# A two-layer diffusion trunk: bias rows laid by the host, counts in five products, gate and residual ahead of the last sums, output in halves from SP, keys moved into a wait

## The chip, the cores and the metric

One core of a Trainium2 chip runs the whole program. Its engines are TensorE (PE in the rows; PEld is its load of weights), VectorE (DVE), ScalarE (ACT), GpSimd (POOL) and SyncE (SP, which only issues transfers and waits). All share 16 DMA engines. The metric is the device time of one execution in microseconds; lower is better.

## What is computed

Two groups of tokens (128 context, 256 latent, together three tiles of 128) go through two layers with shared weights. Cut to what matters here:

```python
mod = silu(cond) @ w_mod + b_mod           # shift1, scale1, gate1, shift2, scale2, gate2
h = x * (1 + scale1) + shift1
a = gmlp(h @ w_in); b = hyena(h @ w_in)    # b: a long convolution by way of spectra
m = attention(h @ w_in)                    # keys: compressed latents @ mla_wukv, and a rotary part
x = layer_norm(ALPHA * x + gate1 * (concat(a, b, m) @ w_out))
h = x * (1 + scale2) + shift2              # then top-1 of 4 groups, top-2 of its 8 experts
x = layer_norm(ALPHA * x + gate2 * moe(h))
```

The outputs are x of both groups and, of each layer, the compressed keys of the context tokens.

## The kernel before

Nothing schedules the program: each engine's order is written out by hand, in one function an engine, and semaphores join them. Everything is float32; a product is two records on TensorE in the trace.

**Weights.** SP streams chunks of 1 MB (`w_mod`, `w_in`, `w_out`) through a ring of four places; a place comes free when TensorE has used it (`chunk_done`). In the expert stage it streams 48 chunks of 2 MB a layer through five slots; a slot comes free when TensorE (`done`) has used it and VectorE and ScalarE have copied a part of it (`copied_d`, `copied_a`).

**Start.** TensorE multiplies the first eight `w_mod` chunks, between them the small products of the filter networks (`filter_hidden`), which VectorE and ScalarE finish. VectorE then adds `b_mod`, loaded by ScalarE's queue into four partition rows of `mod_sums`, to the sums (`add_group(0)`), normalises the third tile of x, shapes the filter taps (`filter_taps`), and TensorE turns those into spectra (L604). ScalarE stores the sums to DRAM, and GpSimd reads them back as broadcast rows for `modulated`.

**Attention.** `keys(g)` (L751) makes the keys of two heads from `ckvT`. In both layers keys 0 and 1 stand behind `forward(1)`, keys 2 and 3 behind `inverse(1)`, ahead of the queries (L796). `inverse` (L746) waits for VectorE.

**Router.** VectorE picks two experts a token. TensorE counts, with a triangular and an all-ones matrix, how many earlier tokens chose each expert (L921), and all tokens (L924). From that VectorE makes the places (`pick`), and TensorE gathers the rows of each expert group (L938).

**Experts.** They come in four octs. In each, `gate_up` (L959) multiplies eight chunks, ScalarE applies silu, VectorE multiplies (`gate`, L1955), TensorE turns the blocks (`turns`), ScalarE copies them out (L1381, L1383), and `down` (L959) multiplies four chunks in two halves of 512 columns. ScalarE and VectorE split the result in a high and a low part (`y_high`, `y_rest`), `scatter` (L1047) brings them back to token order, and VectorE adds them to `moe` (`summed`, L1989). The down chunks of an oct are used among the gate chunks of the next; those of the last oct stand alone (`last_oct_work`). VectorE also copies the chosen parts of each chunk (`copy(c)`, L1949) in between.

**End of a layer.** Tile by tile VectorE multiplies `moe` by the gate (L2178), adds ALPHA x (L2179), takes the statistics (L1535 to L1538), and with ScalarE's square root and row scaling (`norm`, L1225) in between applies the next modulation in layer 0, or the last gain and bias in layer 1 (L1551, L1552). GpSimd stores the three tiles of x (L564).

A branch, taken when an expert has very many tokens, works off the rest of them; with these inputs the other side runs.

Of the kernel before, what the change touches and what calls it, by code (L numbers as in the profile page):

```python
# [199 lines left out]
def build(nc, a, outs):  # L200
# [126 lines left out]
    for name in ("x_in", "cond_in", "mlp_in", "taps_in", "dft_in", "cT", "mod_zero", "bmod_in", "mod_sum", "mod_out", "mod0_out",  # L327
                 "ln_var", "ln_std", "ln_scale", "normed", "pool_step", "x0", "chunk_done", "small_in", "cache_in",
                 "mod12_in", "gate_in", "ln_in", "dve_step", "state_out", "y_out", "h_hi", "h_lo", "h_saved"):
# [50 lines left out]
    def _(sp):  # L380
# [8 lines left out]
        for l in range(DEPTH):  # L389
# [41 lines left out]
            with sp.If(units >= P + 1):  # L431
# [11 lines left out]
                sp.wait_ge(r["multiplied"], REST_MUL * ROUNDS * OCTS)  # L443


    @block.gpsimd
    def _(pool):
# [113 lines left out]
        for t in range(TT):  # L561
            pool.wait_ge(s["x2"], at("x2", DEPTH - 1, t + 1))
            dst = outs[0][0] if t == 0 else outs[1][0, (t - 1) * P:t * P]
            pool.dma_start(dst, x[:, t, :]).then_inc(s["y_out"], 16)  # L564
        pool.wait_ge(s["state_out"], 16 * 2 * DEPTH)
        pool.wait_ge(s["h_saved"], 16 * DEPTH)
        pool.wait_ge(s["y_out"], 16 * TT)
# [3 lines left out]
    def _(pe):  # L571
# [80 lines left out]
        for l in range(DEPTH):  # L652
# [97 lines left out]
            def keys(g):  # L750
                pe.matmul(ps[g][:, :], wukv[:, P * g:P * (g + 1)], ckvT, start=True, stop=True).then_inc(s["k_raw"], 1)  # L751
# [22 lines left out]
            for t in range(4):  # L774
                mm = pe.transpose(ps[1][0:QK, t * P:(t + 1) * P], kpeb[:, t, :], ident)
# [31 lines left out]
            def scores(hh):  # L807
                b = 2 * (hh % 2)
                pe.wait_ge(s["kT"], at("kT", l, 2 if hh == 0 else 4))
# [50 lines left out]
            keys(2)  # L860
            keys(3)
# [57 lines left out]
            for t in range(TT):  # L919
# [278 lines left out]
    def _(act):  # L1198
# [324 lines left out]
    def _(dve):  # L1523
# [111 lines left out]
        for l in range(DEPTH):  # L1635
# [437 lines left out]
            def last_oct_work():  # L2073
# [11 lines left out]
                for i in range(3, BLOCKS):  # L2085
                    y_rest(last_oct, i)
# [214 lines left out]
```

## Time and profile before

| | us |
|---|---|
| median of three runs | 1203.7 |
| the three runs | 1197.64, 1203.7, 1204.4 |
| the profiled execution | 1202.92 |
| its span, first to last instruction | 1201.1 |
| TensorE busy in the span | 1016.5 (85%) |
| VectorE busy | 543.5 (45%) |
| ScalarE busy | 349.3 (29%) |
| read from HBM | 303.11 MB, 257 GB/s |

The times below are from the start of the span. A busy share is a mean over stages; what a change is worth is read at the place where it acts. A row names line, engine, operation, the tile written and those read, the shape, how many records, and in brackets how long the engine was idle before and what ended that.

### The profile page before, as it was taken

How to read it: one execution, taken by the hardware profiler on the slowest of the kernel's cores; microseconds unless marked ns; L12 is line 12 of the kernel's file. 1: busy time of each engine (PE TensorE's matmuls, PEld its weight loads, DVE VectorE, ACT ScalarE, POOL GpSimd, SP SyncE). 2: the span in 40 equal slices, each digit the busy share in tenths (PEclk: the TensorE clock that was granted, in tenths of full speed). 3: DMA queues.
4: the chain of work that ended last, by engine and by line, in shares of the span. 5: the costliest groups of instructions: out<-in, count | busy, mean ns of one | idle time of the engine just before them, and what ended most of it. 6: DMA issues, size and time to landing. Idle time of an engine off the chain costs nothing.

```text
span 1201.1 us, 19792 instructions
## 1 busy us (share of the span) xinstructions
PE 1016.5 (85%) x8178; PEld 600.0 (50%) x8178; DVE 543.5 (45%) x1218; ACT 349.3 (29%) x731; POOL 87.5 (7%) x97
## 2 busy tenths in 40 slices
PE   3768878899977999999986899799959999999970
PEld 2447548765444644435332757565445545344330
DVE  5450033468464234251467615677463242432446
ACT  3120000336131342333242122345122433333331
POOL 1110000010140000000001600000230000000000
PEclk8579988999977999899997899899968999998995
DMA  9865768850356869899986314010486699999941
GB/s 343 320 262 208 294 277 298 327 195 19 140 219 241 348 278 422 337 403 387 424 356 237 140 62 150 12 53 22 168 292 254 244 374 422 367 419 357 408 178 53
DMA packets 48620, 309.52 MB, mean 258 GB/s; under 512 B 6428, under 2 KB 6685, under 8 KB 15749
## 3 DMA queue, kind: packets, MB, share of 16 engines
q1 hardware_dynamic: 39516, 274.08, 57.3%
q0 software_dynamic: 7856, 31.85, 7.5%
q10 hardware_dynamic: 1144, 2.19, 0.6%
q8 instruction: 68, 1.11, 0.4%
q14 instruction: 36, 0.29, 0.1%
HBM read 303.11 MB, written 4.98 MB: 257 GB/s over the span
## 4 chain that ended last, share of the span: by engine, by line
PE 68%; DVE 13%; DMA 11%; ACT 3%; issue 3%; ACTq 1%; SPq 0%; DVEq 0%; POOL 0%
PE bank L959 20%; PE bank L938 9%; PE bank L853 7%; PE bank L694 5%; PE bank L1047 5%; PE bank L680 4%; DMA arena<-in_b_mod 4%; PE bank L705 3%; DMA ring<-in_w_in 2%; DMA ring<-in_moe_gate_up 2%; PE bank L746 2%; PE bank L604 2%; DMA ring<-in_w_mod 2%; PE bank L621 1%; PE bank L796 1%
## 5 line engine op out<-in xcount | busy, mean ns | idle before, releaser
L938 PE MATMUL bank<-sel,h_hi 128*128 128x384 f32 x192 | 83.8, 436 | 9.4 <-DVE sel L1917 9.4
L621 PE MATMUL bank<-ring,arena 128*32 128x64 f32 x3072 | 58.9, 239 | 31.8 <-DMA ring<-in_w_mod 21.4
L853 PE MATMUL bank<-ring,act_t 128*128 128x512 f32 x192 | 84.1, 594 | 0.0
L938 PEld LDWEIGHTS bank<-sel,h_hi 128*128 128x128 f32 x192 | 64.4, 335 | 29.5 <-issue 23.3
L938 PE MATMUL bank<-sel,h_lo 128*128 128x384 f32 x192 | 78.9, 411 | 0.0
L1369 ACT ACTIVATE arena<-bank 128x384 f32<-128x384 f32 x64 | 31.4, 491 | 160.2 <-PE bank L938 160.2
L959 PE MATMUL bank<-ring,arena 128*32 128x512 f32 x480 | 62.4, 640 | 16.5 <-DVE act_t L1955 11.3
L621 PEld LDWEIGHTS bank<-ring,arena 128*32 128x32 f32 x3072 | 52.4, 122 | 45.0 <-issue 22.2
L694 PE MATMUL bank<-act_t,ring 128*128 128x384 f32 x192 | 65.7, 504 | 3.8 <-DMA ring<-in_w_in 3.8
L1047 PE MATMUL bank<-y_hi,selT 128*128 128x512 f32 x144 | 61.7, 428 | 7.0 <-DVE y_lo L1978 6.7
L938 PEld LDWEIGHTS bank<-sel,h_lo 128*128 128x128 f32 x192 | 65.2, 340 | 0.0
L1978 DVE SCALAR_TENSOR_TENSOR y_lo<-bank,region_v,y_hi 128x512 fp32r<-128x512 f32 x48 | 34.6, 748 | 57.3 <-ACT y_hi L1391 57.3
L853 PEld LDWEIGHTS bank<-ring,act_t 128*128 128x128 f32 x192 | 35.8, 190 | 43.6 <-issue 43.6
L1047 PE MATMUL bank<-y_lo,selT 128*128 128x512 f32 x144 | 56.8, 394 | 0.0
L1955 DVE TENSOR_TENSOR act_t<-bank,act_t 128x256 f32<-128x256 f32 x24 | 8.9, 419 | 104.7 <-ACT act_t L1377 104.6
L959 PE MATMUL bank<-arena 128*32 128x512 f32 x416 | 52.0, 598 | 3.1 <-DVE arena L1949 3.1
L1391 ACT ACTIVATE y_hi<-bank,region_v 128x512 fp32r<-128x512 f32 x48 | 31.0, 680 | 75.2 <-PE bank L959 75.2
L694 PEld LDWEIGHTS bank<-act_t,ring 128*128 128x128 f32 x192 | 37.6, 197 | 30.5 <-DMA ring<-in_w_in 4.2
L1047 PEld LDWEIGHTS bank<-y_hi,selT 128*128 128x128 f32 x144 | 26.9, 187 | 50.9 <-DVE y_lo L1978 30.9
L680 PE MATMUL bank<-ring,act_t 128*128 128x256 f32 x192 | 43.9, 391 | 3.8 <-DMA ring<-in_w_in 2.2
L1617 DVE TENSOR_TENSOR arena<-arena,bank 128x512 f32<-128x512 f32 x6 | 4.1, 685 | 87.2 <-PE bank L621 76.4
L959 PE MATMUL bank<-region_k,arena 128*32 128x512 f32 x352 | 42.4, 599 | 0.0
(310 smaller groups left out, 1758.3 us busy)
## 6 DMA issues: line engine op xcount, KB each, us to landing
ring<-in_moe_gate_up SPq DMA_DIRECT2D x60, 1024.0 KB, 8.8
ring<-in_w_mod SPq DMA_DIRECT2D x48, 1024.0 KB, 9.2
region_k<-in_moe_gate_up SPq DMA_DIRECT2D x44, 1024.0 KB, 8.1
ring<-in_moe_down SPq DMA_DIRECT2D x32, 1024.0 KB, 9.5
arena<-in_moe_down SPq DMA_DIRECT2D x28, 1024.0 KB, 9.2
arena<-in_moe_gate_up SPq DMA_DIRECT2D x20, 1024.0 KB, 9.9
ring<-in_w_in SPq DMA_DIRECT2D x10, 1024.0 KB, 7.7
ring<-in_w_out SPq DMA_DIRECT2D x8, 1024.0 KB, 5.2
```

The source lines that it names most:

```text
L604: mm = pe.matmul(ps[SPEC_BANKS[l][b][part]][:, :], dft[:, o:o + P], src[:, t, :], start=(i == 0), stop=(i == len(tiles) - 1))
L621: mm = pe.matmul(ps[MOD_BANK[g]][32 * j:32 * j + 32, c * 64:c * 64 + 64], cT[:, k, :], w[:, k, j * 64:j * 64 + 64], start=(k == 0), stop=( ...
L680: mm = pe.matmul(ps[t][:, c * 256:(c + 1) * 256], act_t[:, k, t * P:(t + 1) * P], w[:, k, :], start=(k == 0), stop=(k == K8 - 1))
L694: mm = pe.matmul(ps[3 + c % 4][:, 0:TOK], w[:, k, c % 2 * P:c % 2 * P + P], act_t[:, k, :], start=(k == 0), stop=(k == K8 - 1))
L705: mm = pe.matmul(ps[t][:, c0 - 1280:c0 - 1280 + n], act_t[:, k, t * P:(t + 1) * P], w[:, k, :], start=(k == 0), stop=(k == K8 - 1))
L853: mm = pe.matmul(ps[2 * t + half][:, :], act_t[:, 2 * c + k, t * P:(t + 1) * P], w[:, k, half * 512:(half + 1) * 512], start=(c == 0 and k ...
L938: mm = pe.matmul(ps[gather_bank(o, k)][:, 0:TOK], src[:, t, k:D:K8], sel[:, t, :, :].rearrange("p v n -> p (v n)"), start=(t == 0 and i == ...
L959: return pe.matmul(out[r, :], stationary[:, r], moving, start=start, stop=stop, tile_position=(0, UNIT * j), skip_group_check=True)
L1047: mm = pe.matmul(ps[SUM_BANKS[t]][:, :], selT[:, v, t * P:(t + 1) * P], y[:, n % 2, :], start=(v == 0 and j == 0), stop=(v == 2 and j == 1 ...
L1369: act.activation(xg[:, first:first + VISITS, k, :], ps[gather_bank(o, k)][:, 0:TOK].rearrange("p (v n) -> p v n", n=P), ACT.Copy)\
L1391: act.activation(y_hi[:, n % 2, :], ps[4 + n % 2][:, :], ACT.Copy, scale=column(o, i % VISITS)).then_inc(e["y_high"], 1)
L1978: dve.scalar_tensor_tensor(y_lo[:, n % 2, :], ps[4 + n % 2][:, :], rt[:, weight:weight + 1], y_hi[:, n % 2, :].bitcast(F32), ALU.mult, ALU ...
```

## The change

**1. Bias rows.** The host lays `b_mod` out as four rows of 3072 numbers. Two DMAs with 4 rows each take the place of four DMAs with 96 runs of 64 numbers each.

**2. Counts.** One triangular product for tile 0; one all-ones product of tile i for all later tiles and the total at once (96, 64, 32 columns, the moving operand repeated); one triangular product for tiles 1 and 2.

**3. Gate and residual.** `folded(t)` multiplies what is summed so far (three octs) by the gate and adds ALPHA x, among the last gate chunks of oct 3. The last oct's sums are multiplied by the gate as they leave the bank, and `residual` adds them to x in halves. The statistics of the first half are taken before the sums of the second.

**4. Output.** In layer 1 the last gain and bias run in halves (`last_affine`), and SP stores each half tile.

**5. Keys.** In layer 1 alone keys 0 and 1 move ahead of `inverse(0)`, keys 2 and 3 to where 0 and 1 were, all in banks 0 and 1; the rotary part goes through bank 7. ScalarE copies keys 0 and 1 out before `signal_out(1)`.

```diff
-        for l in range(DEPTH):
-            bview = a["b_mod"][l].rearrange("(b j n) -> j b n", j=4, n=64)
-            for c in range(2):
-                act.dma_start(mod_sums[c:P:32, l * 1536:(l + 1) * 1536].rearrange("p (b n) -> p b n", n=64),
-                              bview).then_inc(s["bmod_in"], 16)
+        for c in range(2):
+            act.dma_start(mod_sums[c:P:32, :], a["b_mod"]).then_inc(s["bmod_in"], 16)
...
-            for t in range(TT):
-                for i in range(t + 1):
-                    pe.matmul(ps[7][:, t * EXPERTS:(t + 1) * EXPERTS], tri if i == t else ones, chosen[:, i, :],
-                              start=(i == 0), stop=(i == t))
+            counts = ps[7][:, 0:(TT + 1) * EXPERTS].rearrange("p (t n) -> p t n", t=TT + 1)
+            pe.matmul(counts[:, 0, :], tri, chosen[:, 0, :], start=True, stop=True, skip_group_check=True)
             for i in range(TT):
-                mm = pe.matmul(ps[7][:, TT * EXPERTS:(TT + 1) * EXPERTS], ones, chosen[:, i, :], start=(i == 0), stop=(i == 2))
+                pe.matmul(counts[:, i + 1:TT + 1, :], ones, chosen[:, i:i + 1, :].to_broadcast([P, TT - i, EXPERTS]),
+                          start=(i == 0), stop=(i == TT - 1), skip_group_check=True)
+            mm = pe.matmul(counts[:, 1:TT, :], tri, chosen[:, 1:TT, :], start=False, stop=True, skip_group_check=True)
...
+                    if o == OCTS - 1:
+                        last = dve.tensor_tensor(dst, bank[:, :], gates[:, min(t, 1), half * 512:(half + 1) * 512], ALU.mult)
...
+            def folded(t):
...
+                link(dve.tensor_tensor(moe[:, t, :], moe[:, t, :], gates[:, min(t, 1), :], ALU.mult))
+                link(dve.scalar_tensor_tensor(x[:, t, :], x[:, t, :], ALPHA, moe[:, t, :], ALU.mult, ALU.add))
+
+            def residual(t, half):
+
+                cols = slice(half * 512, (half + 1) * 512)
+                dve.wait_ge(e["acc"], SUMS * (OCTS * l + OCTS - 1) + TT * half + t + 1)
+                link(dve.tensor_tensor(x[:, t, cols], x[:, t, cols], moe[:, t, cols], ALU.add))
...
+            def joint(t):
+
+                lnst = st[:, 80 + 14 * t:94 + 14 * t]
+                link(half_stats(t, 1))
+                link(dve.bn_aggr(lnst[:, 12:14], lnst[:, 0:12]))
+                dve.tensor_scalar(st[:, 60 + t:61 + t], lnst[:, 13:14], LN_EPS, None, ALU.add).then_inc(s["ln_var"], 1)
...
+        for t in range(TT):
+            dst = outs[0][0] if t == 0 else outs[1][0, (t - 1) * P:t * P]
+            for half in range(2):
+                cols = slice(half * 512, (half + 1) * 512)
+                sp.wait_ge(s["y_done"], 2 * t + half + 1)
+                sp.dma_start(dst[:, cols], x[:, t, cols]).then_inc(s["y_out"], 16)
+        sp.wait_ge(s["y_out"], 16 * 2 * TT)
...
-            pe.wait_ge(s["latT"], at("latT", l, 2))
+            pe.wait_ge(s["latT"], at("latT", l, 3))
+            if l > 0:
+                keys(0)
+                keys(1)
             inverse(0)
             pe.wait_ge(s["yc"], at("yc", l, 2))
             pe.wait_ge(s["latT"], at("latT", l))
+            if l > 0:
+                pe.wait_ge(s["kT"], at("kT", l, 2))
             signal_turned(1)
             late(l, 3)
             forward(1)
-            keys(0)
-            keys(1)
+            keys(2 * l)
+            keys(2 * l + 1)
```

Three places show what moves. On TensorE the counts of a layer, before (`cst` holds both matrices, `region_v` the choices):

```order
L921 MATMUL bank<-region_v,cst 128x32 [waits oh]
L921 MATMUL bank<-region_v,cst 128x32 x5
L924 MATMUL bank<-region_v,cst 128x32 x3
```

And in the change:

```order
L929 MATMUL bank<-region_v,cst 128x32 [waits oh]
L931 MATMUL bank<-region_v,cst 128x96
L931 MATMUL bank<-region_v,cst 128x64
L931 MATMUL bank<-region_v,cst 128x32
L933 MATMUL bank<-region_v,cst 128x64
```

Nine products become five, three of them wider, and the one wait stays.

On VectorE among the last gate chunks of layer 0, before (a copy is two rows; `small` and `arena` on the left of an L1949 row are its stages, `region_s` is `moe`, L2033 and L2035 prepare the next layer's rows, L1955 is the gate of the last oct):

```order
L2033 TENSOR_TENSOR wukv<-wukv,region_w 128x1024
L1949 REGISTER_ALU [waits e_over,moe_full1,dve_step]
L1949 COPY small<-arena 128x512
L1949 REGISTER_ALU
L1949 COPY small<-arena 128x512
L2035 SCALAR_TENSOR_TENSOR region_q<-region_q,lnr 128x1024
L1949 REGISTER_ALU [waits e_over,moe_full2,dve_step]
L1949 COPY arena<-ring 128x512
L1949 REGISTER_ALU
L1949 COPY arena<-ring 128x512
L1955 TENSOR_TENSOR act_t<-bank,act_t 128x256 [waits e_silu] x3
```

And the same place of the change (line numbers are those of the changed kernel; L2021 and L2022 are `folded`):

```order
L2082 TENSOR_TENSOR wukv<-wukv,region_w 128x1024
L2021 TENSOR_TENSOR region_s<-region_s,arena 128x1024 [waits gate_in,x1,e_acc,dve_step]
L2022 SCALAR_TENSOR_TENSOR x<-x,region_s 128x1024 [waits dve_step]
L1969 REGISTER_ALU [waits e_over,moe_full1,dve_step]
L1969 COPY small<-arena 128x512
...
L2021 TENSOR_TENSOR region_s<-region_s,arena 128x1024 [waits dve_step]
L2022 SCALAR_TENSOR_TENSOR x<-x,region_s 128x1024 [waits dve_step]
L1969 REGISTER_ALU [waits e_over,moe_full2,dve_step]
L1969 COPY arena<-ring 128x512
...
L2021 TENSOR_TENSOR region_s<-region_s,arena 128x1024
L2022 SCALAR_TENSOR_TENSOR x<-x,region_s 128x1024 [waits dve_step]
L1975 TENSOR_TENSOR act_t<-bank,act_t 128x256 [waits e_silu,dve_step]
```

Six operations of 1024 columns now stand ahead of the last gate, two of them ahead of the copy into `small`, four ahead of the copy into `arena`.

On VectorE behind the last scatter of layer 0, before:

```order
L1978 SCALAR_TENSOR_TENSOR y_lo<-bank,region_v,y_hi 128x512 [waits e_y_high,e_w_col] x3
L1989 TENSOR_TENSOR region_s<-bank,region_s 128x512 [waits e_sct] x3
L2158 UNCONDITIONAL_BRANCH
L2178 TENSOR_TENSOR region_s<-region_s,arena 128x1024 [waits ln_in,x1,gate_in,e_acc]
L2179 SCALAR_TENSOR_TENSOR x<-x,region_s 128x1024 [waits dve_step]
```

And in the change:

```order
L1998 SCALAR_TENSOR_TENSOR y_lo<-bank,region_v,y_hi 128x512 [waits e_y_high,e_w_col] x2
L2028 TENSOR_TENSOR x<-x,region_s 128x512 [waits e_acc]
L2028 TENSOR_TENSOR x<-x,region_s 128x512 [waits e_acc,dve_step] x2
L1998 SCALAR_TENSOR_TENSOR y_lo<-bank,region_v,y_hi 128x512 [waits e_y_high,e_w_col,dve_step]
L2032 BN_STATS st<-x 128x6
L2032 BN_STATS st<-x 128x6 [waits dve_step] x2
L2010 TENSOR_TENSOR region_s<-bank,arena 128x512 [waits e_sct,dve_step]
L2010 TENSOR_TENSOR region_s<-bank,arena 128x512 [waits e_sct] x2
L2028 TENSOR_TENSOR x<-x,region_s 128x512 [waits e_acc]
L2028 TENSOR_TENSOR x<-x,region_s 128x512 [waits e_acc,dve_step] x2
L2032 BN_STATS st<-x 128x6 [waits dve_step]
```

The residuals of the first half stand ahead of the last low part, and all three tiles are summed and added before the first statistics are complete; no operation of 1024 columns stands between the sums and the statistics any more.

## Rows read from the trace of the kernel before

**Rows 1.** The page: TensorE's granted clock in 40 slices; the chain by line.

```profile
PEclk8579988999977999899997899899968999998995
...
PE bank L959 20%; PE bank L938 9%; PE bank L853 7%; PE bank L694 5%; PE bank L1047 5%; PE bank L680 4%; DMA arena<-in_b_mod 4%; PE bank L705 3%; DMA ring<-in_w_in 2%; DMA ring<-in_moe_gate_up 2%; PE bank L746 2%; PE bank L604 2%; DMA ring<-in_w_mod 2%; PE bank L621 1%; PE bank L796 1%
```

**Rows 2.** Timeline, VectorE: start us, us, line, operation, idle before.

```profile
48.95 0.69 DVE L1617 TENSOR_TENSOR arena<-arena,bank 128x512 f32<-128x512 f32 x1 [10.77 <-DMA arena<-in_b_mod]
49.55 0.66 DVE L1580 TENSOR_SCALAR arena<-bank,fw 64x384 f32<-64x384 f32 x1
```

**Rows 3.** Timeline, TensorE: the start, and L604 in layer 1.

```profile
41.90 1.54 PE L581 MATMUL bank<-arena,fw 64*64 64x384 f32 x2
...
68.66 11.79 PE L604 MATMUL bank<-region_k,arena 128*128 128x512 f32 x20 [11.12 <-DVE region_k L1599]
...
690.28 8.75 PE L604 MATMUL bank<-region_k,arena 128*128 128x512 f32 x20
```

**Rows 4.** DMA from 13 to 48 us, ScalarE's queue: packets, MB, share.

```profile
q10 hardware_dynamic: 403, 0.11, 1.4%
```

**Rows 5.** Timeline, GpSimd: the modulation rows, the last store.

```profile
52.26 0.53 POOL L468 DMA_DIRECT2D wukv<-mod_rows  x1 [28.19 <-DMA mod_rows<-arena]
...
1191.54 0.53 POOL L564 DMA_DIRECT2D out<-x  x1 [1.86 <-DVE x L1552]
```

**Rows 6.** Transfers to the outputs, 16 to 512 KB, from issue to landing.

```profile
DMA to landing us min/median/max: 1.7/2.9/6.3
```

**Rows 7.** The program's end (L2189): ns min/median/max, start us.

```profile
L2189 SPq DRAIN  x1: 73/73/73, 1169.3 to 1169.3; - x1
...
L2189 POOLq DRAIN  x1: 6194/6194/6194, 1194.7 to 1194.7; - x1
```

**Rows 8.** Timeline, TensorE: router and counts of layer 0.

```profile
353.89 3.63 PE L898 MATMUL bank<-small,act_t 128*128 128x36 f32 x16 [0.69 <-ACT act_t L1346]
362.43 2.77 PE L921 MATMUL bank<-region_v,cst 128*128 128x32 f32 x12 [4.92 <-DVE region_v L1870]
365.01 1.47 PE L924 MATMUL bank<-region_v,cst 128*128 128x32 f32 x6
```

**Rows 9.** Timeline, VectorE: sums behind the last scatter of layer 1, last operation.

```profile
1168.66 1.89 DVE L1989 TENSOR_TENSOR region_s<-bank,region_s 128x512 f32<-128x512 f32 x3 [0.82 <-PE bank L1047]
...
1190.02 1.23 DVE L1552 TENSOR_TENSOR x<-x,lnr 128x1024 f32<-128x1024 f32 x1
```

**Rows 10.** Timeline, VectorE: copies c+10, c+11 and the last gate, layer 0.

```profile
607.81 0.76 DVE L1949 COPY small<-arena 128x512 f32 x2
...
609.83 0.76 DVE L1949 COPY arena<-ring 128x512 f32 x2
...
612.50 1.22 DVE L1955 TENSOR_TENSOR act_t<-bank,act_t 128x256 f32<-128x256 f32 x3 [1.91 <-ACT act_t L1377]
```

**Rows 11.** Timeline, TensorE: `down(3, 0)` and `down(3, 1)` of layer 0.

```profile
615.48 1.92 PE L959 MATMUL bank<-ring,region_w 128*32 128x512 f32 x16 [0.65 <-ACT act_t L1383]
...
618.61 1.92 PE L959 MATMUL bank<-region_k,region_w 128*32 128x512 f32 x16 [0.67 <-DMA region_k<-in_moe_down]
```

**Rows 12.** Timeline, ScalarE: row scaling at layer 1's end.

```profile
1179.32 1.24 ACT L1225 ACTIVATE x<-x,st 128x1024 f32<-128x1024 f32 x1 [4.26 <-DVE st L1545]
```

**Rows 13.** Timeline, all engines: the same place of layer 1.

```profile
1136.14 0.76 DVE L1949 COPY arena<-ring 128x512 f32 x2 [3.78 <-DMA ring<-in_moe_gate_up]
...
1141.02 1.15 ACT L1410 ACTIVATE small<-ring 128x512 f32 x2 [1.64 <-DMA ring<-in_moe_down]
...
1142.98 1.94 PE L959 MATMUL bank<-ring,region_w 128*32 128x512 f32 x8 [2.03 <-ACT act_t L1383]
```

**Rows 14.** Timeline, TensorE: both `inverse`, the queries of layer 1.

```profile
762.91 6.84 PE L746 MATMUL bank<-arena,region_v 128*128 128x128 f32 x24 [4.04 <-DVE region_v L1735]
...
781.44 6.14 PE L746 MATMUL bank<-arena,region_v 128*128 128x128 f32 x24 [2.46 <-DVE region_v L1735]
...
789.13 2.74 PE L796 MATMUL bank<-arena,region_w 128*128 128x384 f32 x8
```

More of the change, by code:

```diff
@@ L858, in w_out @@
                 return mm
-            keys(2)
-            keys(3)
+            if l == 0:
+                keys(2)
+                keys(3)
             pe.wait_ge(s["yc"], at("yc", l))
@@ L1552, in affine, with last_affine @@
             dve.tensor_tensor(x[:, t, :], x[:, t, :], lnr[:, 1, :], ALU.add).then_inc(s[done], 1)
+        def last_affine(base, t):
+            dve.wait_ge(s["normed"], base + t + 1)
+            for half in range(2):
+                cols = slice(half * 512, (half + 1) * 512)
+                link(dve.tensor_tensor(x[:, t, cols], x[:, t, cols], lnr[:, 0, cols], ALU.mult))
+                dve.tensor_tensor(x[:, t, cols], x[:, t, cols], lnr[:, 1, cols], ALU.add).then_inc(s["y_done"], 1)
         def modulated(half, t, done, base=None):
@@ L2069, in oct_work @@
                 fuse(4)
+                if o == OCTS - 1:
+                    folded(0)
                 copy(c + 10)
                 fuse(5)
+                if o == OCTS - 1:
+                    folded(1)
                 copy(c + 11)
+                if o == OCTS - 1:
+                    folded(2)
             def last_oct_work():
@@ L2084, in last_oct_work @@
                 copy(c + 3)
-                for i in range(3, BLOCKS):
-                    y_rest(last_oct, i)
+                y_rest(last_oct, 3)
+                y_rest(last_oct, 4)
+                for t in range(TT):
+                    residual(t, 0)
+                y_rest(last_oct, 5)
+                for t in range(TT):
+                    link(half_stats(t, 0))
                 summed(last_oct, 1)
+                for t in range(TT):
+                    residual(t, 1)
             for o in range(1, OCTS - 1):
@@ L2098, in _, with chained @@
                 count = [0]
+                def chained(ins):
+                    count[0] += 1
+                    ins.then_inc(r["picked"], 1)
+                    dve.wait_ge(r["picked"], count[0])
+                chained(dve.memset(region_s[:], 0.0))
                 for turn in range(ROUNDS * OCTS):
@@ L2157, in _ @@
                 dve.wait_ge(r["summed"], REST_SUMMED * ROUNDS * OCTS)
+                for t in range(TT):
+                    chained(dve.tensor_tensor(moe[:, t, :], moe[:, t, :], gates[:, min(t, 1), :], ALU.mult))
+                    chained(dve.tensor_tensor(x[:, t, :], x[:, t, :], moe[:, t, :], ALU.add))
+                    chained(half_stats(t, 0))
+                for t in range(TT):
+                    joint(t)
             with dve.Else():
@@ L2161, in _ @@
                 last_oct_work()
-            dve.wait_ge(e["acc"], SUMS * OCTS * (l + 1))
-            dve.wait_ge(s["gate_in"], 32 * (2 * l + 2))
+                for t in range(TT):
+                    joint(t)
             dve.wait_ge(s["ln_in"], 32 * (2 * l + 3))
-            dve.wait_ge(s["x1"], at("x1", l))
             base = norms(l, 2, 0)
@@ L2173, in normed_use @@
                 else:
-                    affine(base, t, "x2")
-            for t in range(TT):
-                link(dve.tensor_tensor(moe[:, t, :], moe[:, t, :], gates[:, min(t, 1), :], ALU.mult))
-                link(dve.scalar_tensor_tensor(x[:, t, :], x[:, t, :], ALPHA, moe[:, t, :], ALU.mult, ALU.add))
-                norm_stats(t)
-                if t >= 1:
-                    norm_scale(base, t - 1)
-                if t >= 2:
-                    normed_use(t - 2)
+                    last_affine(base, t)
+            norm_scale(base, 0)
+            norm_scale(base, 1)
+            normed_use(0)
             norm_scale(base, TT - 1)
```

47 lines of the change are left out of this document (26 added, 21 removed).

## Prediction

> **What bounds the kernel now.** I read the chain that ended last first. TensorE carries most of it, yet one transfer, `arena<-in_b_mod`, is 4% alone [rows 1]. So the question is at which ends TensorE waits, and I read the timelines there: the start, the router, the last oct of each layer, the keys of layer 1, the end.
>
> At the start VectorE stands 10.77 us before its first `add_group` because `b_mod` has not landed; then `filter_hidden(1, 1)` follows at 49.55 [rows 2]. TensorE has given `filter_hidden(1, 1)` its product by 41.90 + 1.54 = 43.44, and later stands 11.12 us before the spectra (L604) [rows 3]. The late transfer moves little: queue 10 has 403 packets for 0.11 MB between 13 and 48 us [rows 4]. At the end nothing computes after VectorE's last add: GpSimd issues the store at 1191.54 [rows 5], a store of its size lands 2.9 us later [rows 6], and GpSimd then spends 6194 ns in a DRAIN [rows 7].
>
> **b_mod.** 384 runs of 64 numbers become 8 runs of 3072. At the old rate (403 packets in 35 us) eight take under 1 us, so the biases land near 14 us, long before they are needed; the price of the load becomes nothing, hidden by the mod products. `add_group(0)` then follows the eighth chunk, which TensorE ends at 41.9, and `filter_hidden(1, 1)` follows its product at 43.45 instead of 49.55: 6.1 us. Late next is that product. The whole goes through: TensorE's 11.12 us before L604 is longer than 6.1, and GpSimd, which loads the modulation rows at 52.26 once the sums are stored [rows 5], does so about 6 us sooner too; VectorE uses them only behind the taps that L604 waits for, so not before 68.6 [rows 3]. Bounds: 5 (another load lands with it) to 9 (L604 took 11.79 us, partly at half clock (1.2 of 2.4 GHz), and 8.75 in layer 1 [rows 3]). I take **6.1**.
>
> **Counts.** 9 products of 32 columns become 5 of 32, 96, 64, 32 and 64. The 18 records (two a product) ran from 362.43 to 366.48, 0.225 us each. Records of 36 columns took 3.63/16 = 0.227, so width is not the price [rows 8]. 10 records: 2.3 to 2.5 us. VectorE's places and then the gathers wait for them. Saved: 4.05 - 2.4 = 1.65 a layer, bounds 0.9 (96 columns cost three times 32) to 1.9; **3.3** for both. The expert stream keeps it, since its slots come free at TensorE's pace.
>
> **Gate and residual ahead, layer 0.** Three `folded(t)` of two 1024-wide operations (1.23 each [rows 9], 0.03 for the chained wait) are 2.52 us each, put behind the copies c+9, c+10 and before the last gate. VectorE is not idle enough. It ended copy c+9 and `fuse(4)` at 607.7 and began c+10 at 607.81 and c+11 at 609.83, the gates at 612.50 [rows 10]. Now c+10 begins at 610.3, c+11 at 614.9, and the gates at 618.1, ending 619.3. Behind the gates stand `turns`, ScalarE's copy of the transposed blocks, then TensorE's `down(3, 0)`: about 619.7, 620.3, 620.35 instead of 615.48; `down(3, 1)` comes 2.3 us later, at 622.7 instead of 618.61 [rows 11], where a transfer had been the last to arrive. So +4.1, and nothing later absorbs it: the rest is a chain TensorE, ScalarE, VectorE.
>
> Behind the last scatter (its first tile ready at R): before, gate, residual, statistics and affine followed the sums tile by tile. The twelve long operations of this tail are the same in both layers, and in layer 1 they ended at R + 22.6: R is 1168.66, the last one ends at 1190.02 + 1.23 [rows 9]. Now VectorE does three half residuals in the wait for `y_high(5)`; three half statistics push the sums 1.3 us past R; sums 1.89, residuals 2.2, three `joint` 3.05, then the norms. (A 512-wide operation is 1.89/3 = 0.63 unchained [rows 9], and I take 0.7 chained and 0.1 to 0.3 for those of one to twelve columns.) ScalarE's 1.24 for a row block [rows 12] alternates with them: scale 0 at R + 8.5, scale 1 at +10.2, h complete at +18.2. Gain 4.45. Net for layer 0: 4.45 - 4.1 = **0.35**.
>
> **The same in layer 1.** Here loads are later: c+11 landed at 1136.1 and the first down chunk at 1141.0, and TensorE began `down(3, 0)` at 1142.98 behind ScalarE, which had that copy to do first [rows 13]. With the folds c+11 is copied at 1137.65, the gates run 1140.9 to 1142.1, ScalarE turns at 1142.2 and TensorE starts at 1143.1: **-0.1**. Without that cover it costs the 4.1 of layer 0. Behind the scatter the same reordering, R = 1168.66: scale 1 at 1178.9, then `last_affine` in halves, four operations 2.7 instead of 2.4 for two, three times, with one scale of 0.35 between: last half at 1187.65, where it was 1191.25. **3.6**.
>
> **Keys.** Layer 1 moves keys 0 and 1 into TensorE's 4.04 us before `inverse(0)`; keys 2 and 3 take their old place, and the pair just ahead of the queries goes. But `query(0)` also waits for the convolution: VectorE ends it near 788.85, so it starts at 788.9 instead of 789.13 [rows 14]: 0.25. More may come from the clock: `inverse(0)` took 6.84 us, the same 24 records 6.14 the next time, after a shorter wait [rows 14]. Filling half the wait gives 0 to 2.3; I take 0.75, together **1.0**. ScalarE's extra copies lie in its idle time; the new wait on `kT` ends 5 us early.
>
> **Output.** Six half tiles from SP instead of three from GpSimd. From the last add to the end it was 1201.1 - 1191.25 = 9.85: 0.29 to issue, 2.9 to land, then the DRAIN 6.19 and the closing barrier [rows 5 to 7]. GpSimd's last transfer is now one of layer 1's middle, so it drains while the others work. From SP: the last half is 256 KB; landing between 1.7 and 2.9 [rows 6], I take 2.5, plus 0.05 before and 0.4 of barrier: 3.0. **6.85**. In front of the last half on SP stand five others, each issued as it is made, 1.3 us apart. The Trainium skill, "DMA: Bandwidth & Descriptors", Specifications, gives a first-byte latency of about 1 us on GpSimd's path and 0.6 on SP's. By that alone the move would be worth 0.4 and the sum about 1188; the DRAIN row is why I don't follow it.
>
> **Sum.** 6.1 + 3.3 + 0.35 - 0.1 + 3.6 + 1.0 + 6.85 = 21.1 from the profiled execution's 1202.92: **1181.8 us**. The median of the three runs is 0.8 above that execution. About 1% (12 us) is what a measurement of this kernel can tell from no change.
>
> **Rivals.**
> *Fold uncovered in layer 1 too.* For it: in layer 0 the loads came before VectorE was ready. Against: the rows of layer 1 show two arrivals late. 1181.8 + 4 = 1185.8. Chance 0.15.
> *The DRAIN is not GpSimd's own.* If closing costs 6.2 us whichever engine stores last, 1188. For: no second case in the trace; against: SP's own DRAIN took 73 ns [rows 7]. Chance 0.12.
> *The start keeps another wait*, say the modulation rows: 1187.9. The 16 us from issue to use speak against; it needs a load slower than any store that is timed here (6.3 us at most [rows 6]). 0.06.
> *The clock gives back more.* Shorter waits before L604 and `inverse(0)`, and earlier gathers, each partly at half clock: up to 2.9 + 1.5 + 1; or layer 0's loads land late enough to cover part of the fold. 1177. The profile shows half clock only around TensorE's waits. 0.15. The Trainium skill, "TensorE: Matmul & The Clock Gate", Loop structure matters more than you think, says that unbroken matmuls keep the clock and long waits lose it; this trace agrees where `inverse(0)` follows 4.04 us of waiting [rows 14].
> *Slower.* The order of the waits shifts so that TensorE is granted the half clock in the expert stages. Between 375 and 640 and 905 and 1143 it works nearly without a wait; its clock row reads 8 or 9 tenths of full speed in nearly all slices [rows 1]. Half clock doubles the work done in it, so 42 us more of it cost 21 us, and above that the kernel is slower. Nothing in the change idles TensorE there by more than 2 us at a time but for the 4 us at layer 0's end: 0.02, 1205.
> The forecast keeps 0.5; its own range is 1178 to 1185.
>
> **Range.** 1174 (clock gains together with a covered fold) to 1190 (DRAIN stays, fold partly uncovered): some 1 in 10 left out. Faster by over 1% needs under 1191.7: all cases but two failing together and the last: 0.93; within 1% 0.05; slower 0.02.
>
> **What would show it.** Right: no wait of VectorE for `b_mod`, L604 near 62.6; 10 records of counts and about 2.4 us; in layer 0 `gate` 5.6 us later against copy c+9 than before, `down(3, 1)` waiting for ScalarE and not for a transfer; in layer 1 the same distance as before; from R to VectorE's last add 19.0 instead of 22.6; 3 us from there to the end, GpSimd's long DRAIN over long before. Wrong: a copy c+11 in layer 1 that did not wait for its load; a long DRAIN on SP; a wait for modulation rows before h.

## Result

| | before | after |
|---|---|---|
| median | 1204.54 (14 runs) | 1189.1 (14 runs) |
| lowest, highest | 1197.2, 1210.43 | 1180.41, 1202.02 |
| ratio, 95% interval | 1 | 0.988 (0.985 to 0.991) |
| profiled execution, its span | 1202.92, 1201.1 | 1187.77, 1186.0 |

The change saves 14.5 us (10.7 to 18.2), of 21.1 that were forecast. The time lies 7.3 us above the forecast and inside the range, just under its upper end. The same kernel measured again on another chip gave 0.9875 (0.982 to 0.993). Executions of one kernel differ by over 20 us here (the changed one ran in 1180.41 to 1202.02), so a single trace shows places well and sums badly.

### The profile page after: what moved, and what is told of

Same layout as the page of the kernel before. It is cut to its first block and busy times, and to the rows that moved or that the text cites. A ratio compares the mean times of both kernels' runs of the same rounds, so it can differ in the third digit from the quotient of the medians.

```text
span 1186.0 us, 19792 instructions
## 1 busy us (share of the span) xinstructions
PE 1015.1 (86%) x8162; PEld 594.2 (50%) x8162; DVE 554.1 (47%) x1236; ACT 349.2 (29%) x731; POOL 86.1 (7%) x94
## 5 line engine op out<-in xcount | busy, mean ns | idle before, releaser
L947 PEld LDWEIGHTS bank<-sel,h_hi 128*128 128x128 f32 x192 | 64.6, 337 | 29.6 <-issue 23.3
L861 PEld LDWEIGHTS bank<-ring,act_t 128*128 128x128 f32 x192 | 35.9, 190 | 43.5 <-issue 43.5
L697 PEld LDWEIGHTS bank<-act_t,ring 128*128 128x128 f32 x192 | 37.9, 199 | 30.6 <-DMA ring<-in_w_in 4.3
L683 PE MATMUL bank<-ring,act_t 128*128 128x256 f32 x192 | 44.8, 397 | 6.7 <-issue 3.7
L683 PEld LDWEIGHTS bank<-ring,act_t 128*128 128x128 f32 x192 | 38.2, 200 | 12.7 <-issue 3.9
```

The lines of the kernel that those rows point to most:

```text
L683: mm = pe.matmul(ps[t][:, c * 256:(c + 1) * 256], act_t[:, k, t * P:(t + 1) * P], w[:, k, :], start=(k == 0), stop=(k == K8 - 1))
L697: mm = pe.matmul(ps[3 + c % 4][:, 0:TOK], w[:, k, c % 2 * P:c % 2 * P + P], act_t[:, k, :], start=(k == 0), stop=(k == K8 - 1))
L861: mm = pe.matmul(ps[2 * t + half][:, :], act_t[:, 2 * c + k, t * P:(t + 1) * P], w[:, k, half * 512:(half + 1) * 512], start=(c == 0 and k ...
L947: mm = pe.matmul(ps[gather_bank(o, k)][:, 0:TOK], src[:, t, k:D:K8], sel[:, t, :, :].rearrange("p v n -> p (v n)"), start=(t == 0 and i == ...
```

## The profile after, place by place

Line numbers are now those of the changed kernel. First the clock row of the page, then VectorE's and TensorE's timelines at the start (start us, duration, line, operation, idle before and what ended it). They answer [rows 2] and [rows 3].

```profile
PEclk9589979999978989999987799999978999999997
```

```profile
42.62 0.69 DVE L1637 TENSOR_TENSOR arena<-arena,bank 128x512 f32<-128x512 f32 x1 [3.75 <-PE bank L624]
43.96 0.67 DVE L1600 TENSOR_SCALAR arena<-bank,fw 64x384 f32<-64x384 f32 x1 [0.65 <-PE bank L584]
...
63.07 7.28 PE L607 MATMUL bank<-region_k,arena 128*128 128x512 f32 x12 [5.66 <-DVE region_k L1619]
```

VectorE no longer waits for `b_mod` but for TensorE, and the spectra begin at 63.07 instead of 68.66: 5.6 us (forecast 6.1). The clock row is a little fuller in the early slices and has its low slices elsewhere.

TensorE's timeline in the router of layer 0 answers [rows 8].

```profile
354.18 0.64 PE L929 MATMUL bank<-region_v,cst 128*128 128x32 f32 x2 [4.92 <-DVE region_v L1890]
354.63 1.47 PE L931 MATMUL bank<-region_v,cst 128*128 128x96 f32 x6
355.91 0.67 PE L933 MATMUL bank<-region_v,cst 128*128 128x64 f32 x2
```

The 10 records take 356.58 - 354.18 = 2.40 us where 18 took 4.05: 1.65, as forecast, and in both layers.

TensorE's timeline in the middle of layer 1 answers [rows 14].

```profile
754.56 1.99 PE L754 MATMUL bank<-arena,wukv 128*128 128x512 f32 x4 [0.25 <-ACT arena L1295]
758.25 4.61 PE L749 MATMUL bank<-arena,region_v 128*128 128x128 f32 x24 [1.70 <-DVE region_v L1755]
...
765.78 6.27 PE L738 MATMUL bank<-arena 128*128 128x256 f32 x20 [0.74 <-ACT arena L1285]
...
775.45 4.61 PE L749 MATMUL bank<-arena,region_v 128*128 128x128 f32 x24 [1.68 <-DVE region_v L1755]
...
781.36 2.85 PE L804 MATMUL bank<-arena,region_w 128*128 128x384 f32 x8 [1.30 <-DVE act_t L1765]
```

Keys 0 and 1 fill the wait, and both `inverse` take 4.61 us instead of 6.84 and 6.14. From the first `inverse` to the queries it was 789.13 - 762.91 = 26.2 us and is 23.1, and the first `inverse` is not later for the keys ahead of it: 3.1 us against the 1.0 forecast. The queries now wait for VectorE, as the 0.25 of the forecast had it; most of the rest is the clock. It was at 1.2 GHz for part of both `inverse` before, worth 3.8 us, and it is so now for part of `forward(1)` between them (L738), which takes 6.27 us instead of 4.58 and loses 1.7 of that.

VectorE's timeline at the last gate chunks of layer 0 answers [rows 10], TensorE's the same place and [rows 11].

```profile
594.50 1.23 DVE L2021 TENSOR_TENSOR region_s<-region_s,arena 128x1024 f32<-128x1024 f32 x1
595.76 1.23 DVE L2022 SCALAR_TENSOR_TENSOR x<-x,region_s 128x1024 f32<-128x1024 f32 x1
...
602.34 1.22 DVE L2021 TENSOR_TENSOR region_s<-region_s,arena 128x1024 f32<-128x1024 f32 x1
603.59 1.22 DVE L2022 SCALAR_TENSOR_TENSOR x<-x,region_s 128x1024 f32<-128x1024 f32 x1
604.85 1.09 DVE L1975 TENSOR_TENSOR act_t<-bank,act_t 128x256 f32<-128x256 f32 x3
```

```profile
597.94 1.07 PE L968 MATMUL bank<-small,arena 128*32 128x512 f32 x8 [1.77 <-DVE small L1969]
...
602.48 1.07 PE L968 MATMUL bank<-arena 128*32 128x512 f32 x8 [1.75 <-DVE arena L1969]
605.42 1.26 PE L1001 MATMUL bank<-cst,act_t 128*128 128x128 f32 x6 [1.88 <-DVE act_t L1975]
...
607.54 3.64 PE L968 MATMUL bank<-ring,region_w 128*32 128x512 f32 x16
...
612.05 3.64 PE L968 MATMUL bank<-region_k,region_w 128*32 128x512 f32 x16
```

The folds stand in VectorE's way as forecast: TensorE waits for it three times, and the gates come 604.85 - 592.58 = 12.3 us after copy c+9 (592.58 was its start), where they came 612.50 - 605.79 = 6.7 after it: 5.6 us, the number of the forecast. What it had not: both halves of the down products take 3.64 us instead of 1.92, at 1.2 GHz, after three waits in a row. From copy c+9 to the first scatter of the last oct it is 617.37 - 592.58 = 24.8 us, where it was 622.19 - 605.79 = 16.4.

All engines at the start of layer 1:

```profile
659.38 2.55 POOL L471 TENSOR_TENSOR x<-x,lnr 128x1024 f32<-128x1024 f32 x1 [4.01 <-ACT act_t L1253]
...
659.65 2.56 DVE L1619 TENSOR_TENSOR region_k<-region_v 128x256 f32<-128x256 f32 x1
...
662.31 2.05 PE L683 MATMUL bank<-ring,act_t 128*128 128x256 f32 x4 [3.69 <-issue]
...
685.72 8.75 PE L607 MATMUL bank<-region_k,arena 128*128 128x512 f32 x20
```

VectorE's last operation of the second tile's filter taps (L1619) takes 2.56 us where its fellows before it take 0.42; it ends 0.3 us after GpSimd's operation of 2.55 us has ended. The code lets the first product with `w_in` (L683) wait for these taps, and it begins 0.1 us after them, 3.69 us after TensorE's last work. In the trace of before, L680 waited 0.66 us at this place. From the first transpose of h to the spectra (L607; L604 in the kernel before) it is 685.72 - 653.54 = 32.2 us, where it was 690.28 - 662.86 = 27.4. So of the 9.3 us that the kernel was ahead by at the transposes, 4.7 are gone at the spectra: 2.1 by that operation, 2.6 by the clock that follows TensorE's wait (the first 20 records of the input products take 6.8 us instead of 4.2).

The end: VectorE's sums behind the last scatter and its last operation, which answer [rows 9], and the DRAINs of the last line, which answer [rows 7].

```profile
1165.92 1.89 DVE L2010 TENSOR_TENSOR region_s<-bank,arena 128x512 f32<-128x512 f32 x3
...
1182.83 0.69 DVE L1572 TENSOR_TENSOR x<-x,lnr 128x512 f32<-128x512 f32 x1
```

```profile
L2253 POOLq DRAIN  x1: 5949/5949/5949, 895.6 to 895.6; - x1
...
L2253 SPq DRAIN  x1: 13/13/13, 1185.7 to 1185.7; - x1
```

The last scatter group begins 4.0 us earlier than before, the last addition ends at 1183.5 instead of 1191.25, so 3.7 more (forecast 3.6), and from there to the end it is 2.5 us instead of 9.85: 7.35 (forecast 6.85). GpSimd drains for 5.9 us in the middle of the program, where nobody waits for it.

So in this pair of traces 11.1 of 15.1 us come from the end, and only 4.0 are left at the last scatter of the 10.7 forecast up to there. The experiments ask where they went.

## Experiments

Each ratio is to the kernel before, timed in five rounds on the same chip beside it, with its 95% interval. A hundredth is 12 us.

**Part 3 taken back.** The functions `folded`, `residual` and `joint` go, in both layers; the end of a layer is that of before.

```diff
-                if o == OCTS - 1:
-                    folded(0)
                 copy(c + 10)
...
```

> The changed kernel with part 3 (gate and residual ahead) taken back in both layers; bias rows, counts, keys and the output in halves from SP stay. Theory A (the folds are what fell short: they hold VectorE up behind the last gate chunks of layer 0 by 5.6 us, and TensorE then ran the last two down products at half clock, 3.6 us instead of 1.9 each): the tails grow back by 4.5 and 3.7 us, the delay and the half clock of layer 0 go (8.4 us), so about 1189 us, no different from the changed kernel, and both down products of oct 3 take 1.9 us a half. Theory B (the stream of expert weights swallowed what was won before it, the folds cost what was forecast): tails 8.2 back, fold 4.1 off, about 1193 us.

Ratio 0.9895 (0.984 to 0.995), against 0.988: by the two ratios part 3 is worth 1.8 us of the whole change, where 3.85 were forecast, with an interval of some 7 us either way. TensorE in layer 0:

```profile
612.66 1.22 PE L1001 MATMUL bank<-cst,act_t 128*128 128x128 f32 x6 [0.26 <-DVE act_t L1975]
...
614.92 1.92 PE L968 MATMUL bank<-ring,region_w 128*32 128x512 f32 x16 [0.50 <-ACT act_t L1395]
...
618.03 1.92 PE L968 MATMUL bank<-region_k,region_w 128*32 128x512 f32 x16 [0.64 <-DMA region_k<-in_moe_down]
```

The short waits and the 1.92 of before are back, as theory A said. The interval does not part it from theory B.

**Part 3 alone.** The kernel before with it, output from GpSimd.

```diff
-                    last = dve.tensor_tensor(dst, bank[:, :], dst, ALU.add) if o else dve.tensor_copy(dst, bank[:, :])
+                    if o == OCTS - 1:
+                        last = dve.tensor_tensor(dst, bank[:, :], gates[:, min(t, 1), half * 512:(half + 1) * 512], ALU.mult)
...
```

> The kernel before with part 3 alone (gate and residual ahead of the last sums, statistics of the first half ahead; output in whole tiles from GpSimd as before). Forecast: 0.35 + 3.5 us less. Theory A: nothing gained, 0 to 3 us either way, since in layer 0 the folds cost 5.6 us and up to 3.4 more by half clock in down(3, 0) and down(3, 1), against 4.5 and 3.7 won in the tails; the trace shows VectorE's gates of oct 3 in layer 0 directly behind the third fold, and TensorE's waits of about 1.8 us ahead of its last three groups there.

Ratio 1.0001 (0.997 to 1.003): no change, where 3.85 us were forecast. TensorE's timeline:

```profile
609.35 1.06 PE L959 MATMUL bank<-arena 128*32 128x512 f32 x8 [1.76 <-DVE arena L1949]
612.29 1.53 PE L992 MATMUL bank<-cst,act_t 128*128 128x128 f32 x6 [1.88 <-DVE act_t L1955]
...
614.68 3.64 PE L959 MATMUL bank<-ring,region_w 128*32 128x512 f32 x16
...
667.69 4.61 PE L680 MATMUL bank<-ring,act_t 128*128 128x256 f32 x10 [3.43 <-issue]
```

Both marks of the changed kernel stand in it: the waits with a slow down product behind them, and the wait of 3.4 us ahead of the input products of layer 1.

**GpSimd behind the taps.** The changed kernel with one wait more on GpSimd, in layer 1.

```diff
                 pool.wait_ge(s["hT"], at("hT", l))
+                pool.wait_ge(s["filt_eo"], at("filt_eo", l))
                 for t in range(TT):
                     affine(t, "x2")
```

> The changed kernel in which GpSimd, before the gain and bias on x at the start of layer 1, waits for all filter taps of VectorE. In the changed kernel one tap operation of VectorE took 2.56 us instead of 0.42 while GpSimd's operation of 2.55 us ran, TensorE stood 3.7 us and then ran the first input products at half clock (6.9 us more than needed for none, 3.4 lost). Theory C (the two engines hinder each other): that operation takes 0.42 us again, TensorE's wait goes from 3.7 to about 1.6 us, and with the clock kept about 5 us less, 1184 us; with the clock still lost 2 us less, 1187 us. Rival (TensorE's wait is another's, such as a load of w_in): no change of the wait, 1189 us.

Ratio 0.9851 (0.980 to 0.990), against 0.988: 3.5 us by the two ratios, with an interval of some 7 us either way, so the times alone don't show it. The trace is clear (VectorE, TensorE, GpSimd):

```profile
659.27 0.42 DVE L1620 TENSOR_TENSOR region_k<-region_v 128x256 f32<-128x256 f32 x1
...
659.79 4.55 PE L684 MATMUL bank<-ring,act_t 128*128 128x256 f32 x20 [1.53 <-ACT act_t L1254]
...
663.13 2.34 POOL L471 TENSOR_TENSOR x<-x,lnr 128x1024 f32<-128x1024 f32 x1 [8.15 <-DVE region_k L1620]
```

No operation of the taps is slow any more, TensorE's wait is 1.53 us, and it keeps the full clock. All 14 traces agree on what the slow tap costs. I took the distance from TensorE's first transpose of h in layer 1 to the spectra. It is 27.4 or 27.5 us in the seven in which that tap took 0.42 us, the four kernels with this wait and three without it, and 32.1 to 34.7 in the seven in which it took 2.55 to 2.58. The changed kernel stands among these with 32.2: the slow tap costs it 4.7 us.

What decides is whether GpSimd begins ahead of that tap, which is due 6.1 us after the first transpose. In the three kernels that go without the wait and without harm GpSimd began 6.4 to 6.7 us after it, in the seven others 5.6 to 6.1. In the trace of before it missed by little: the tap ended at 669.39 and GpSimd began at 669.43.

**Part 3 alone, with that wait; and that wait alone.** The same line in the kernel before with and without part 3.

> The kernel before with part 3 (gate and residual ahead) and with GpSimd's gain and bias of layer 1 behind the filter taps. Part 3 alone gave a ratio of 1.000. If the hindrance between GpSimd and VectorE at the start of layer 1 is what ate its gain, the ratio is 0.995 to 0.997 (2.1 us of the tap operation and up to 3.4 us of half clock back). If the folds' delay in layer 0 ate it, 1.000 again.

Ratio 0.9927 (0.989 to 0.997), against 1.0001 for part 3 alone. The two intervals just miss each other: with the hindrance gone, part 3 and the wait together save 8.8 us (4.1 to 13.4).

```profile
668.26 6.93 PE L681 MATMUL bank<-ring,act_t 128*128 128x256 f32 x31 [1.33 <-ACT act_t L1248]
```

> The kernel before with only GpSimd's gain and bias of layer 1 behind the filter taps. In its trace GpSimd's operations already slow taps down (2.56 us instead of 0.42), but the later ones, which only the spectra wait for, and TensorE has 21 us of input products ahead of those. So if the hindrance costs only where the first four taps are hit: no difference, 0.999 to 1.001. If slow taps cost in any place: some us less, 0.996.

Ratio 0.9985 (0.995 to 1.002): for the kernel before the wait alone brings nothing that can be told. So the hindrance takes about what part 3 gives. In all five kernels with part 3 and without the wait the tap is hit. But it is not part 3's alone: of the five others without the wait it is hit in two, bias rows alone and keys alone, which take 34.7 and 34.5 us from the transpose to the spectra. GpSimd starts when ScalarE has the last transposed block of h; that this comes sooner when TensorE runs the transposes at the full clock is my reading, and no run was made to show it.

**Folds where VectorE waits.** The changed kernel with the folds cut into halves of 512 columns; `folded` takes a half and waits for the sums of that half.

```diff
                 copy(c + 7)
+                if o == OCTS - 1:
+                    folded(0, 0)
                 y_rest(o - 1, 3)
                 y_rest(o - 1, 4)
+                if o == OCTS - 1:
+                    folded(1, 0)
+                    folded(2, 0)
...
-                if o == OCTS - 1:
-                    folded(0)
                 copy(c + 10)
...
                 y_rest(last_oct, 1)
+                folded(0, 1)
+                folded(1, 1)
                 y_rest(last_oct, 2)
...
                 copy(c + 3)
+                folded(2, 1)
```

> The changed kernel with the folds cut in halves of 512 columns and put where VectorE waits: the first half of each tile behind copy c+7 and behind the fifth low part of the oct before, the second half behind the second and in front of the fourth low part of the last oct. Theory A: the gates of oct 3 follow copy c+11 as in the kernel before, the last down products of layer 0 run at full clock, the tails keep their gain: 5 to 8 us less than the changed kernel, about 1182 us. Theory B: no more than the 4.1 us forecast for the fold, less what the stream swallows in layer 1: 1185 to 1189 us.

Ratio 0.9818 (0.975 to 0.989), 7.5 us under the changed kernel by the two ratios, with intervals that overlap. VectorE's copy c+11 and gate of layer 0, then TensorE in both layers:

```profile
595.59 0.76 DVE L1969 COPY arena<-ring 128x512 f32 x2 [1.01 <-DVE region_q L2085]
598.02 1.22 DVE L1975 TENSOR_TENSOR act_t<-bank,act_t 128x256 f32<-128x256 f32 x3 [1.66 <-ACT act_t L1389]
```

```profile
598.59 1.22 PE L1001 MATMUL bank<-cst,act_t 128*128 128x128 f32 x6 [0.25 <-DVE act_t L1975]
...
602.37 3.52 PE L968 MATMUL bank<-ring,region_w 128*32 128x512 f32 x16 [2.02 <-ACT act_t L1395]
...
1128.03 3.52 PE L968 MATMUL bank<-ring,region_w 128*32 128x512 f32 x16 [2.04 <-ACT act_t L1395]
```

The gates are where they were, but the expectation that the down products would keep the full clock fell. With VectorE out of the way the first down chunk is late in layer 0 too, ScalarE has to copy it first, TensorE waits 2.0 us and the product takes 3.52 us all the same.

**Both edits.**

> The changed kernel with both edits of the call before: folds in halves where VectorE waits, and GpSimd's gain and bias of layer 1 behind the filter taps. If the folds' place and the hindrance between GpSimd and VectorE are two separate losses, their gains add: about 9 us below the changed kernel, 1180 us, a ratio of 0.978. If the stream of expert weights takes back what is won ahead of it in layer 1, no better than the spread folds alone: 1184 us.

Ratio 0.9754 (0.971 to 0.980), median 1176.38: 29.6 us under before, about 15 under the changed kernel, and its interval lies clear of that one's. Within the noise that is what two separate losses would give: the edits brought 3.5 and 7.5 us one by one, 11 together, with intervals of 7 us and more either way. The wait on GpSimd has now been put into three kernels that the slow tap hits; by ratio it gave 3.5, 8.9 and 7.7 us, and 1.8 in the kernel before, which was not hit.

**The output from GpSimd again.** The changed kernel, its six half stores moved from SP to GpSimd.

```diff
-                sp.dma_start(dst[:, cols], x[:, t, cols]).then_inc(s["y_out"], 16)
+                pool.dma_start(dst[:, part], x[:, t, part]).then_inc(s["y_out"], 16)
```

> The changed kernel with the six half stores issued by GpSimd instead of SP, nothing else. If the DRAIN of about 6 us belongs to GpSimd after a store of its own, it stands at the end again: from VectorE's last addition to the end 9 to 10 us instead of 2.5, about 1196 us. If the forecast's rival holds (closing costs it whichever engine stores last) no difference: 1189 us.

Ratio 0.9915 (0.987 to 0.996), against 0.988: 4 us, of the right sign and within the interval. GpSimd's last issue, and its DRAIN:

```profile
1193.01 0.54 POOL L566 DMA_DIRECT2D out<-x  x1 [0.79 <-DVE x L1571]
```

```profile
L2252 POOLq DRAIN  x1: 6439/6439/6439, 1195.6 to 1195.6; - x1
```

From VectorE's last addition (1192.7) to the end (1202.2) it is 9.5 us, against 2.5 with SP in the same kernel. The DRAIN is GpSimd's own: 7.0 us for the place of the stores. That rival is out.

**The other parts alone.**

> The kernel before with part 1 alone (bias rows laid by the host, two DMAs). Forecast: 6.1 us less, ratio 0.995, VectorE's first add_group near 42 us and L604 near 62.6. If the stages behind swallow what is won at the start: the trace shows L604 6 us earlier all the same, but the experts of layer 1 end less than 3 us earlier.

Ratio 0.9956 (0.992 to 0.999): 5.3 us (0.8 to 9.7), with 6.1 forecast inside. VectorE's first `add_group`, and L604:

```profile
42.60 0.69 DVE L1614 TENSOR_TENSOR arena<-arena,bank 128x512 f32<-128x512 f32 x1 [3.69 <-PE bank L621]
```

```profile
63.06 10.56 PE L604 MATMUL bank<-region_k,arena 128*128 128x512 f32 x20 [5.81 <-DVE region_k L1596]
```

> The kernel before with part 2 alone (counts in five products). Forecast: 3.3 us less, ratio 0.997, 10 records in about 2.4 us in each layer. If the stream of expert weights, whose rate is the bound in the expert stages, does not start earlier for it: 0.999 to 1.000 although the records are fewer.

Ratio 0.9964 (0.994 to 0.999): 4.3 us, with 3.3 forecast inside. What is saved ahead of the stream of expert weights is kept.

```profile
359.26 0.64 PE L920 MATMUL bank<-region_v,cst 128*128 128x32 f32 x2 [4.92 <-DVE region_v L1870]
359.71 1.47 PE L922 MATMUL bank<-region_v,cst 128*128 128x96 f32 x6
360.99 0.67 PE L924 MATMUL bank<-region_v,cst 128*128 128x64 f32 x2
```

> The kernel before with part 5 alone (keys of layer 1 moved). Forecast: 1.0 us less. The trace shows inverse(0) in layer 1 behind a wait of about 1.7 us instead of 4.0 and at full clock, 4.6 us instead of 6.8: then 2 to 3 us less from the first key to the queries, and a ratio of 0.998, which is within what this measurement tells from none. Rival: the wait only moves to the queries (they wait for VectorE), 0.25 us.

Ratio 0.9973 (0.994 to 1.001): 3.2 us, not told from 1.0 or from none; the trace has the shape that was described.

```profile
772.17 4.61 PE L746 MATMUL bank<-arena,region_v 128*128 128x128 f32 x24 [1.71 <-DVE region_v L1747]
...
788.46 4.61 PE L746 MATMUL bank<-arena,region_v 128*128 128x128 f32 x24 [2.46 <-DVE region_v L1747]
794.38 2.85 PE L801 MATMUL bank<-arena,region_w 128*128 128x384 f32 x8 [1.30 <-DVE act_t L1757]
```

> The changed kernel itself once more, beside these: 0.988 as before (0.985 to 0.991), so that the ratios of the single parts, taken on other chips, can be added against it. The single parts have given 0.9956 (bias), 1.000 (part 3), 0.997 (keys) so far.

Ratio 0.9875. Bias, counts, keys and part 3 alone sum to 12.8 us and the stores' place gave 4 between runs: 17, against 14.5 to 15 for all at once, within the noise of five measurements. Its trace repeats both losses: waits of 1.77, 1.76 and 1.88 us ahead of the last three groups of oct 3 in layer 0, a tap of 2.56 us, and 3.76 us of wait behind it.

**What the early folds cost, over all traces.** The folds begin right behind copy c+9. So I measured from that copy to the first `turns` of the last oct and to the first scatter behind it. Six kernels have the folds there (the changed kernel twice, with the GpSimd wait, with the stores on GpSimd, part 3 alone, the same with the wait), eight have not.

| mean, us | folds early | not early |
|---|---|---|
| layer 0, copy c+9 to `turns` | 12.8 | 7.5 |
| layer 0, copy c+9 to scatter | 23.6 | 18.7 |
| layer 1, copy c+9 to `turns` | 10.3 | 7.6 |
| layer 1, copy c+9 to scatter | 20.3 | 19.7 |

The folds cost 4.9 us in layer 0 and 0.6 in layer 1, with standard errors of 0.7 and 0.5, and so 5.5 in all, near the 7.5 that spreading them gave; behind the first scatter they cost nothing more (18.5 us to the last one in layer 0, with and without). In layer 1 the gates come 2.7 us later and the stretch behind them is 2.1 shorter: there the load of the first down chunk covers most of the delay. The half clock in the down products is no special price of the folds. With them one half at least is slow in 12 of 12 places; without them, where the load makes TensorE wait, in 14 of 16. But the trace of before is one of the two that keep the full clock in layer 0, so the pair of traces shows 8.4 us there.

## The prediction against this

*b_mod, counts.* Right: 5.6 us in the trace and 5.3 (0.8 to 9.7) by time for 6.1; 2.40 us for ten records where 2.3 to 2.5 were forecast. The whole of it went through.

*Output.* Right, with the reason: 7.35 for 6.85 in the traces, and the DRAIN comes back with GpSimd's store. The first-byte latencies of the Trainium skill ("DMA: Bandwidth & Descriptors", Specifications), about 1 us against 0.6, would have made it 0.4; the measurement decides against going by them alone at a program's end.

*Keys.* Mechanism right, size too small: 3.1 us in the pair of traces for 1.0. The mis-sized term is the clock, 0.75 forecast. I had looked at the first `inverse` only, and the second, at 6.14 us, was partly at the half clock as well.

*Folds.* For layer 0 "the gates at 618.1" was right in its distance, and 4.1 in its size: 4.9 over all traces, though 8.4 in this pair. For layer 1 "**-0.1**" was right, and the first rival (uncovered there too) is out.

```profile
1133.68 0.76 DVE L1969 COPY arena<-ring 128x512 f32 x2
```

```profile
1134.50 1.07 PE L968 MATMUL bank<-arena 128*32 128x512 f32 x8 [0.50 <-DVE arena L1969]
1137.44 1.08 PE L1001 MATMUL bank<-cst,act_t 128*128 128x128 f32 x6 [1.88 <-DVE act_t L1975]
```

Counted from copy c+9 (1130.93 before, 1127.13 now) the gates come 9.7 us after it instead of 7.7, and `down(3, 0)` begins 12.1 after it in both. The forecast's list of signs was wrong about this: it wanted the gates at "the same distance as before" and a copy c+11 that waits for its load, while its own working had that copy 1.5 us behind the load and the gates 2.3 later. The copy now stands directly behind the folds, at 1133.68, without a wait.

*Tails.* Right: 22.6 us from R to the end of the last addition became 1183.52 - 1165.92 = 17.6 plus the 1.3 by which R moved, where 19.0 was forecast, and layer 0 gained 4.5 for 4.45.

*The step that failed* is "Net for layer 0: 4.45 - 4.1 = **0.35**". It lets the 4.45 us of the tail go through whole. "Late next" was asked for at the start, but not here: what follows when h of layer 1 is ready 4.5 us sooner. What follows is GpSimd's gain and bias on x, which now runs beside the tap that TensorE waits for. This was put at nothing and took 4.7 us, 2.1 of them as wait and 2.6 by the half clock behind it. With the folds at 4.9, the net of layer 0 was 4.5 - 4.9 - 4.7 = -5.1 us instead of 0.35. That is 5.4 of the 6.6 us (2.9 to 10.4) by which the saving fell short of 21.1. No rival named it, though VectorE's operations of 2.56 us beside GpSimd's stood in the trace of before, a few us later, where nobody waited.

The pair of traces, place by place, with what was forecast:

| us saved in the pair | traces | forecast |
|---|---|---|
| start of the span to the first gather, layer 0 | 9.9 | 7.75 (bias, counts) |
| to copy c+9 | 3.3 | 0 |
| to the last scatter | -8.4 | -4.1 (folds) |
| to the first transpose of h, layer 1 | 4.5 | 4.45 (tail) |
| to the spectra | -4.7 | 0 |
| to the first gather, layer 1 | 4.9 | 2.65 (keys, counts) |
| to copy c+9 | -5.6 | 0 |
| to the last scatter | 0.2 | -0.1 (folds) |
| to the end | 11.1 | 10.45 (tail, output) |

*Luck.* The two stretches from the first gather to copy c+9 hold nothing that was changed. They differ by +3.3 and -5.6 us here and over the 14 traces by 10 and 6 us from the shortest to the longest. The time lies 0.9 us inside the range, with an interval of some 4 us either way, so that it fell inside at all is in part luck too.

*What stays open.* In both traces of the changed kernel the expert stage of layer 1 begins 9.4 and 6.5 us ahead of before, and 5.6 and 5.0 of that are gone at copy c+9, ahead of the folds. These are the two longest of the 14 (233.9 and 233.2 us, the others 227.4 to 231.7). In the expert stage the stream moves 4 MB in about 10 us in either kernel, so a slot that is freed late may not be made up for, and a stretch at half clock may cost for good; no experiment parts these from chance.

## What to carry to other kernels

Work that is moved off a tail onto an engine "with idle time" belongs into that engine's own waits, and cut to their length. Ahead of the last gates the six operations cost 4.9 us in layer 0. Cut into halves and put into waits they left 37.9 and 38.1 us from copy c+9 to the last scatter, against 37.0 in the six kernels with no folds at all, whose standard deviation is 1.8. When a stage is made to end sooner, look at every engine that starts on its result, and at whether GpSimd then runs beside operations of VectorE that somebody waits for. Let the last store of a program go out from an engine whose DRAIN is short: SP's took 13 ns here, GpSimd's 5.9 to 6.4 us.

## What the runs showed of the hardware

An operation of VectorE with two inputs in SBUF stood still while GpSimd ran one of its own: 0.42 us became 2.56 (or 1.61 where it began in the middle of GpSimd's), in all five of their kind that came after GpSimd's first one in the changed kernel, while those between them that read a PSUM bank and SBUF (L1615, L1616) never took over 0.48. With GpSimd behind them all 12 of layer 1 took 0.42. The Trainium skill says this in "SBUF — State Buffer", Terms: VectorE and GpSimd arbitrate for one port pair, held for a whole instruction, and the loser blocks. The trace agrees.

GpSimd's DRAIN at the end of its program took 5.9 to 6.4 us in all 14 traces, wherever it stood: at 895.6, when its last transfer was of layer 1's middle, and at 1195.6, right behind a store. It is hidden only if GpSimd comes to its end before the others.

Widening a product from 32 to 96 columns cost nothing to be seen: six records of 96, 64 and 32 columns in 1.47 us, as six of 32 took before.
